# In-place recurrence operands, and a last layer without the meta tokens' own rows, in a two-layer hybrid encoder on Trainium2

## The chip, the cores and the metric

The program runs on one core of one Trainium2 chip. The metric is the device time in microseconds (us); lower is better. Engines: PE is TensorE (matmuls; PEld its weight loads), DVE VectorE, ACT ScalarE, POOL GpSimd, SP SyncE, which here issues every DMA.

## The reference

512 tokens of width 1024, with 16 learned meta tokens in front (T = 528), pass through two layers. The meta rows of the last layer's output are dropped.

```python
h = jnp.concatenate([meta, x], axis=1)                  # 528 rows
for l in range(DEPTH):                                   # 2 layers
    u = rmsnorm(h, norm_g[l])
    p = u @ w_in[l]                                      # 1024 -> 9216
    hq, hf_f, hf_b, hi, hgt, aq, ak, av, agt = jnp.split(p, split_idx, axis=-1)
    o_h = hgrn2_mixer(hq, hf_f, hf_b, hi, hgt, lbs[l], hg_norm_g[l])
    o_a = diff_attention_mixer(aq, ak, av, agt, diff_lambda[l], diff_subln_g[l], l, cos, sin)
    h = h + jnp.concatenate([o_h, o_a], axis=-1) @ w_out[l]
out = rmsnorm(h, final_norm_g)[:, N_META:]
```

`hgrn2_mixer` is a gated linear recurrence, S_t = diag(f_t) S_{t-1} + k_t v_t^T, o_t = S_t^T q_t, run forwards and backwards over the 528 rows with 8 heads of 128x128 state, k = (1-lb) sigmoid(-z) and f = lb + (1-lb) sigmoid(z). `diff_attention_mixer` is dense attention with 8 heads, each the difference of two softmaxes (components of 64), with rotary positions. Both outputs are normalised and gated.

## The kernel before

Activations stand transposed: features on the 128 partitions, the 528 tokens along the free axis. The work of a layer is cut into **units**, output tiles of 128 features (`layer_units`, L69): per recurrent head zf, zb, q, v, g, per attention head aq, ak, av, ag, and then the output projection in outA, outB and outC. A unit is 8 **pieces** (one per 128 input features); a piece (L1130) is six matmuls in fp32r, for three products of high and low parts of weight and activation (`w_hi*u_hi`, `w_hi*u_lo`, `w_lo*u_hi`), each in two halves of 264 tokens. ACT rounds a weight tile to its high part (L507), POOL takes the rest (L437).

The 16 heads of a layer run one after another, 13 steps each (0 to 12). All five engines have a program of their own written out step by step, and semaphores between them. At each step PE does the head's own matmuls and is then **fed** a set number of pieces of the next head's units (`feed`, L1170; `HG_FEED`, L103, and `AT_FEED`, L104). ACT evacuates a finished unit (`evacuate`, L550) and then rounds the weights of a later one; DVE follows it up (`follow`, L851: for zf and zb L885 and L887 form the gate f; for aq and ak L897 to L905 apply the rotation).

A **recurrent head** has no chunks of 16. Its 528 rows are scored in 8 levels: level 0 is the diagonal, and level lv >= 1 is, within blocks of 2m rows, m = 2^(lv-1), the scores between the two halves of a block. At PE step s, `level` (L1200) does level s-1: four pairs of 128x128 fp32 matmuls (L1210, each two instructions) on keys and queries from `qk_dec`, and for levels 0 to 4 a small 16x16 one for the meta rows (L1207). DVE prepares each level in `level_products` (L938). `decay` holds four rows of running products of gates, two for queries and two for keys:

```python
step(dve.tensor_tensor(block_half(dst, m, 1), block_half(qkk_c[:, 0:3:2, :], m, 1), block_half(decay[:, 0:2, :], m, 1), ALU.mult))
dve.tensor_tensor(block_half(dst, m, 0), block_half(qkk_c[:, 0:2, :], m, 0), block_half(decay[:, 2:4, :], m, 0), ALU.mult)
totals = step(dve.tensor_tensor(totals[...], block_totals(slice(0, 3), m, 0), block_totals(slice(0, 3), m, 1), ALU.mult))
second = step(dve.tensor_tensor(second, second, spread(slice(0, 2), 0), ALU.mult))
firsts = step(dve.tensor_tensor(firsts, firsts, spread(slice(1, 3), 1), ALU.mult))
```

So per level there are two products (L950, L954), the next totals of the gates (L963) and two spreads that widen `decay` (L972, L974); `copy_level` (L916, L922) puts the level's scores under a mask into `score`. The last products are 1056 wide (L1045, L1050). The starting values of `decay` come from ACT (`set_decay`, L541 and L542) and POOL (L447, L448). Level lv's products wait for level lv-2's matmuls, since `qk_dec` has two buffers. Steps 9 to 12 turn the keys, form and chain the states (L976, L987) and compute the outputs (L1274 to L1282); step 12 waits for `mixed` of the head before, which `gate_meta` (L1023) releases.

An **attention head** goes through five chunks of queries, four of 128 rows and one of the 16 meta rows, two components each. At steps 0 to 9 PE forms the scores (L1300, L1302), DVE the maximum (L1064), ACT the exponential (L660), and the next scores wait for it. DVE then combines the two components (`p`, L1092), PE transposes (L1329, L1330) and multiplies by the values (L1315, L1317), ACT reads out and squares. `scale_output` (L1002) multiplies the rows of the head before by the inverse root from POOL (L1006, and L1009 for the meta rows), PE turns them back (L1218, L1222), and `gate_main` and `gate_meta` gate them.

Of the kernel before, what the change touches and what calls it, by code (L numbers as in the profile page):

```python
# [31 lines left out]
P = 128  # L32
DEPTH = 2
# [19 lines left out]
AT_TILES = ("aq", "ak", "av", "ag")  # L53
STAGE_USE = {"zf": 0, "zb": 1, "g": 2, "aq": 0, "ak": 1, "ag": 2}
# [44 lines left out]
HG_STEPS = LEVELS + 5  # L99
AT_STEPS = 2 * 6 + 1  # L100
DECAY_STEP = TURN_KEYS + 1
# [58 lines left out]
def unit_of(tile):  # L160

    return next(i for i, u in enumerate(UNITS) if u[0] == "outB" and u[2] == tile)

# [33 lines left out]
def encoder_trunk(nc, x_t, w_units, norm_g, lb_logits, hg_gain, lambdas, at_gain, final_g,  # L197
# [12 lines left out]
    with ctx:  # L210
# [30 lines left out]
        totals = sb("totals", [P, 3, TOTALS])  # L241
        decay = sb("decay", [P, 4, T])
        qkk = sb("qkk", [P, 2, 3, T])
        qk_dec = sb("qk_dec", [P, 2, 2, T])

# [47 lines left out]
        decay_set = sem("decay_set")  # L293
        qk_ready = sem("qk_ready")
        level_done = sem("level_done")
# [81 lines left out]

        def u_out(k):

            if k < 4:  # L380
                return decay[:, k, N_META:T]
            return qkk[:, (k - 4) // 2, (k - 4) % 2, N_META:T]
# [41 lines left out]
        def _(pool):  # L424
# [16 lines left out]
            def set_decay(l, c):  # L441
                g = l * HG_HEADS + c
                if g > 0:
                    pool.wait_ge(qk_ready, 10 * g)
                if c == 0:
                    pool.wait_ge(h_sq_summed, l + 1)
                pool.memset(decay[:, 1, :], 1.0).then_inc(decay_set, 1)  # L447
                pool.memset(decay[:, 3, :], 1.0).then_inc(decay_set, 1)  # L448

# [11 lines left out]
            def cut_mixed(n):  # L461
                pool.wait_ge(mix_hi_ready, n + 1)
                pool.tensor_tensor(mix_lo[:, n % 8, :], mixed_t[:, :],  # L463
                                   mix_hi[:, n % 8, :].bitcast(f32), ALU.subtract)\
                    .then_inc(mix_lo_ready, 1)
# [3 lines left out]
            for l in range(DEPTH):  # L469
# [7 lines left out]
                set_decay(l, 0)  # L477
                follow(range(len(HG_TILES)))
                for c in range(HEADS):
                    n = l * HEADS + c  # L480
                    for s in range(steps_of(c)):
                        if s == mix_step(c) and c > 0:
                            cut_mixed(n - 1)
                        if s == DECAY_STEP and c + 1 < HG_HEADS:
                            set_decay(l, c + 1)
                        follow(units_after(c, s))
# [7 lines left out]
        def _(act):  # L494
# [15 lines left out]
            def square_h(n, k):  # L510
# [13 lines left out]
                act.activation(decay[:, k % 4, :], h[:, tile, :], ACT.Square).then_inc(h_sq, 1)  # L524

            def root(n):

                act.wait_ge(h_sq_summed, n + 1)
                act.activation(two(sq[:, :]), pair[:, :, both], ACT.Sqrt, bias=eps_count[:, :])\
                    .then_inc(root_ready, 1)  # L530
# [4 lines left out]

            def set_decay(l, c):
                g = l * HG_HEADS + c
                act.wait_ge(stage_read, 3 * (l * HEADS + c) + 2)
                if g > 0:
                    act.wait_ge(qk_ready, 10 * g)  # L540
                act.activation(decay[:, 0:4:2, :], gate_f[:, 0:2, :], ACT.Copy).then_inc(decay_set, 1)  # L541
                act.activation(gate_f[:, 2, :], gate_f[:, 0, :], ACT.Copy).then_inc(decay_set, 1)  # L542
# [7 lines left out]
            def evacuate(l, i):  # L550
# [3 lines left out]
                src = proj[t % 2][:, :, both]  # L554
                act.wait_ge(unit_done, t + 1)
                if what not in ("outA", "outB", "outC"):
# [5 lines left out]
                    a, b = two(stage[:, use % 2, 0, :]), two(stage[:, use % 2, 1, :])  # L562
                    done = evacuated[t % 2]
                    if what in ("zf", "zb"):
# [8 lines left out]
                        act.activation(qkk[:, c % 2, 1 + d, :], stage[:, use % 2, 1, :], ACT.Copy,  # L573
                                       scale=one_minus_lb[:, l, row:row + 1]).then_inc(k_scaled, 1)
                    elif what == "q":
                        act.activation(two(qkk[:, c % 2, 0, :]), src, ACT.Copy).then_inc(done, 1)
# [21 lines left out]
            def scale_output(n):  # L598

                act.wait_ge(o_inv_ready, n + 1)  # L600
                for j in range(N_CHUNKS + 1):
# [3 lines left out]
                    if j < N_CHUNKS:  # L605
# [9 lines left out]

            def hgrn(l, c, s):
# [16 lines left out]
                if s == HG_STEPS - 1:  # L633
                    if n > 0:
                        act.wait_ge(o_turned, 2 * n)
                    act.wait_ge(o_done, g + 1)
                    step(act.activation(o_rows[:, 0:N_CHUNKS, :],
                                        main[:, :].rearrange("p (c n) -> p c n", c=4), ACT.Copy))
                    act.activation(o_rows[0:N_META, N_CHUNKS, :], meta[0:N_META, 0:P], ACT.Copy)\
                        .then_inc(o_taken, 1)  # L640
                    act.wait_ge(o_taken, n + 1)
                    for j in range(N_CHUNKS + 1):
# [4 lines left out]
                        if j < N_CHUNKS:  # L647
# [4 lines left out]
            def attend(l, c, s):  # L652
                n, a = l * HEADS + c, l * AT_HEADS + c - HG_HEADS
                i, comp = s // 2, s % 2
                if i < 5:
                    rows = P if i < 4 else N_META
                    if comp == 0 and i >= 2:
                        act.wait_ge(p_ready, a * 5 + i - 1)
                    act.wait_ge(max_ready, a * 10 + 2 * i + comp + 1)
# [5 lines left out]
                if comp == 0 and 2 <= i < 7:  # L665
                    j = i - 2
                    rows = P if j < 4 else N_META
                    if j == 0:
                        act.wait_ge(o_turned, 2 * n)
                        act.wait_ge(mix_lo_ready, n)  # L670
                    act.wait_ge(pv_done, a * 5 + j + 1)
                    inv = row_inv[0:rows, j % 2, 0:1]
                    act.activation(o_rows[0:rows, j, :], meta[0:rows, 0:P], ACT.Copy, scale=inv)\
                        .then_inc(pv_read if j < 4 else o_taken, 1)
                    if j < 4:
                        act.wait_ge(pv_read, a * 4 + j + 1)
                    else:
# [3 lines left out]
                                   accum_out=o_sums[0:rows, j:j + 1]).then_inc(act_step if j < 4 else sq_ready, 1)  # L681
                    if j < 4:
# [3 lines left out]
                if comp == 1 and 1 <= i < 6:  # L686
                    j = i - 1
                    rows = P if j < 4 else N_META
                    act.wait_ge(p_turned, a * 5 + j + 1)
# [15 lines left out]
            def round_mixed(l, c):  # L705
# [5 lines left out]
                act.activation(mix_hi[:, c % 8, :], mixed_t[:, :], ACT.Copy).then_inc(mix_hi_ready, 1)  # L711
# [10 lines left out]
            for l in range(DEPTH):  # L722
# [6 lines left out]
                for i in range(len(HG_TILES)):  # L729
                    evacuate(l, i)  # L730
                    if i == 2:
                        set_decay(l, 0)
                for c in range(HEADS):
                    for s in range(steps_of(c)):
# [5 lines left out]
                        if s == DECAY_STEP and c + 1 < HG_HEADS:  # L740
                            set_decay(l, c + 1)
# [21 lines left out]
        def _(dve):  # L763
# [53 lines left out]
            def add_squares(n, k):  # L817
# [4 lines left out]
                dve.tensor_tensor(sq[:, :], decay[:, 0, :] if k == 1 else sq[:, :], decay[:, k % 4, :],  # L822
                                  ALU.add).then_inc(h_sq_added, 1)

            def invert_roots(n):
                dve.wait_ge(root_ready, n + 1)
                after(step(dve.reciprocal(sq[:, :], sq[:, :])))
# [23 lines left out]
            def follow(l, i):  # L851
# [4 lines left out]
                if what in ("outA", "outB"):  # L856
                    dve.wait_ge(unit_done, t + 1)
                    dve.tensor_tensor(two(h[:, j, :]), two(h[:, j, :]), proj[t % 2][:, :, both], ALU.add)\
# [4 lines left out]
                if what == "outC":  # L863
                    for tile in range(EARLY_TILES):
# [4 lines left out]
                        else:  # L869
                            dve.wait_ge(unit_done, t + 1)  # L870
                        dve.tensor_tensor(two(h[:, tile, :]), two(h[:, tile, :]),
                                          last_out(l, tile)[:, :, both], ALU.add)\
# [7 lines left out]
                a, b = stage[:, use % 2, 0, :], stage[:, use % 2, 1, :]  # L880
# [8 lines left out]
                elif what == "g":  # L889
                    dve.tensor_tensor(gates[:, c % 2, :], a, b, ALU.mult).then_inc(stage_read, 1)  # L890
                elif what == "ag":
                    dve.scalar_tensor_tensor(gates[:, c % 2, :], a, 1.0, b, ALU.add, ALU.mult)\
                        .then_inc(stage_read, 1)
                else:
# [4 lines left out]
                    step(dve.tensor_tensor(a, a, cos_sin[:, 0, :], ALU.mult))  # L899
                    w = step(dve.tensor_tensor(b, b, cos_sin[:, 1, :], ALU.mult))  # L900
# [4 lines left out]
                    dve.tensor_tensor(gate_f[:, d, :], a, b, ALU.add).then_inc(stage_read, 1)  # L905
# [30 lines left out]
            last_decay = {}  # L936
# [505 lines left out]
```

## Time and profile before

| | |
|---|---|
| median of 3 runs | 1691.0 us (1689.66 to 1691.99) |
| the profiled execution | 1691.08 us, of which 1689.3 us are the span of the trace |
| mean granted PE clock | 0.981 |
| busy: PE, PEld, DVE, ACT, POOL | 1554.6, 1514.3, 1188.7, 754.1, 567.1 us |

The span runs from the first to the last instruction in the trace. Matmuls are pipelined, so the distance between starts tells what one costs and not the length of a row. Line numbers with an L are those of the kernel before.

### The profile page before, as it was taken

What the parts mean: (1) busy time and instruction counts of PE and PEld (TensorE: products, weight loads), DVE (VectorE), ACT (ScalarE), POOL (GpSimd) and SP (SyncE); (2) the same over time, 40 slices, a digit from 0 to 9 for tenths busy, and PEclk for the clock granted to TensorE, in tenths of its full rate; (3) what the DMA queues carried; (4) which work ended last, traced back from release to release, by engine and by line L of the source; (5) the groups of instructions that cost most, each with busy time, mean ns of one, the idle gap of its engine ahead of it and who ended that gap; (6) DMA issues with size and microseconds to landing.
All of it is one profiled execution on the core that took longest, in us unless ns stands there. A gap on an engine that the chain in (4) does not pass through costs nothing.

```text
span 1689.3 us, 30863 instructions
## 1 busy us (share of the span) xinstructions
PE 1554.6 (92%) x12616; PEld 1514.3 (90%) x12616; DVE 1188.7 (70%) x1871; ACT 754.1 (45%) x1712; POOL 567.1 (34%) x319
## 2 busy tenths in 40 slices
PE   5999999999999999999989999999999999999996
PEld 5999998999999999998888899899889999999985
DVE  6888888888734666665468888888895356666655
ACT  5343433333434556655343344343335346665542
POOL 3334332334234333332433333333233233333331
PEclk8999999999999999999999999999999999999998
DMA  4211111111212222222221111111112122222211
GB/s 148 86 51 63 51 51 51 63 51 51 64 63 89 64 74 65 64 64 64 75 76 52 62 51 51 63 51 50 51 51 76 62 90 64 63 72 68 72 56 62
DMA packets 34492, 109.57 MB, mean 65 GB/s; under 512 B 4912, under 2 KB 5040, under 8 KB 34352
## 3 DMA queue, kind: packets, MB, share of 16 engines
q1 hardware_dynamic: 34352, 107.61, 19.9%
q8 instruction: 100, 1.64, 0.4%
q14 instruction: 40, 0.33, 0.1%
HBM read 96.84 MB, written 2.10 MB: 59 GB/s over the span
## 4 chain that ended last, share of the span: by engine, by line
PE 62%; DVE 27%; issue 9%; ACT 1%; POOL 1%; DMA 0%; DVEq 0%; SPq 0%; ACTq 0%
PE proj L1149 41%; DVE qk_dec L954 5%; PE meta L1315 3%; DVE decay L972 3%; PE pair L1210 3%; DVE score L922 3%; DVE stage L885 2%; PE pair L1300 2%; DVE qk_dec L950 2%; PE pair L1302 2%; PE main L1329 2%; DVE o_rows L1009 2%; DVE decay L974 2%; DVE totals L963 2%; PE main L1274 1%
## 5 line engine op out<-in xcount | busy, mean ns | idle before, releaser
L437 POOL TENSOR_TENSOR w_lo<-w_raw,w_hi 128x1024 fp32r<-128x1024 f32 x178 | 453.4, 2548 | 804.1 <-ACT w_hi L507 800.9
L1149 PE MATMUL proj<-u_hi,w_hi 128*128 128x264 f32 x2304 | 503.7, 300 | 15.2 <-DVE u_lo L841 15.2
L1149 PE MATMUL proj<-u_lo,w_hi 128*128 128x264 f32 x2304 | 471.5, 286 | 0.0
L1149 PE MATMUL proj<-u_hi,w_lo 128*128 128x264 f32 x2304 | 471.2, 286 | 0.0
L1149 PEld LDWEIGHTS proj<-u_hi,w_hi 128*128 128x128 f32 x2304 | 360.8, 192 | 18.5 <-issue 16.3
L1149 PEld LDWEIGHTS proj<-u_lo,w_hi 128*128 128x128 f32 x2304 | 361.5, 191 | 0.0
L1149 PEld LDWEIGHTS proj<-u_hi,w_lo 128*128 128x128 f32 x2304 | 360.2, 190 | 0.0
L1064 DVE TENSOR_REDUCE neg_max<-pair 128x1 f32<-128x528 f32 (+1 forms) x160 | 112.3, 702 | 248.6 <-PE pair L1302 248.6
L660 ACT ACTIVATE decay<-pair,neg_max 128x528 f32<-128x528 f32 (+1 forms) x160 | 111.9, 699 | 289.7 <-DVE neg_max L1064 289.7
L507 ACT ACTIVATE w_hi<-w_raw 128x1024 fp32r<-128x1024 f32 x178 | 186.4, 1048 | 13.3 <-PE proj L1149 8.8
L1210 PE MATMUL pair<-qk_dec 128*128 128x128 f32 x896 | 131.8, 292 | 4.2 <-DVE score L922 4.2
L950 DVE TENSOR_TENSOR qk_dec<-qkk,decay 128x528 f32<-128x528 f32 (+1 forms) x112 | 89.4, 799 | 58.0 <-PE meta L1282 51.2
L1210 PEld LDWEIGHTS pair<-qk_dec 128*128 128x128 f32 x896 | 114.3, 199 | 7.8 <-DVE qk_dec L954 4.6
L1149 PE MATMUL proj<-mix_hi,w_hi 128*128 128x264 f32 x496 | 105.3, 293 | 9.4 <-issue 4.7
L463 POOL TENSOR_TENSOR mix_lo<-mixed_t,mix_hi 128x528 fp32r<-128x528 f32 x32 | 42.2, 1319 | 203.9 <-ACT mix_hi L711 203.9
L954 DVE TENSOR_TENSOR qk_dec<-qkk,decay 128x528 f32<-128x528 f32 (+1 forms) x112 | 108.1, 965 | 0.0
L569 ACT ACTIVATE stage<-proj 128x528 f32<-128x528 f32 x32 | 19.6, 611 | 197.6 <-PE proj L1149 197.6
L1149 PE MATMUL proj<-mix_hi,w_lo 128*128 128x264 f32 x496 | 100.8, 285 | 0.0
L1149 PE MATMUL proj<-mix_lo,w_hi 128*128 128x264 f32 x496 | 100.7, 284 | 0.0
L1300 PE MATMUL pair<-k_stack,q_stack 128*128 128x264 f32 (+1 forms) x320 | 86.4, 290 | 13.5 <-ACT decay L660 13.5
L1149 PEld LDWEIGHTS proj<-mix_hi,w_hi 128*128 128x128 f32 x496 | 76.6, 189 | 12.1 <-issue 6.7
L1315 PE MATMUL meta<-v_main,cols 128*128 128x128 f32 x640 | 85.9, 277 | 0.0
(186 smaller groups left out, 2615.2 us busy)
## 6 DMA issues: line engine op xcount, KB each, us to landing
w_raw<-w_units SPq DMA_DIRECT2D x178, 512.0 KB, 3.4
k_stack<-k_stack SPq DMA_DIRECT2D x32, 132.0 KB, 2.3
q_stack<-gate_f SPq DMA_DIRECT2D x32, 132.0 KB, 2.4
h<-x_t SPq DMA_DIRECT2D x8, 264.0 KB, 4.3
out_t<-decay SPq DMA_DIRECT2D x4, 256.0 KB, 2.1
out_t<-qkk SPq DMA_DIRECT2D x4, 256.0 KB, 2.1
cos_sin<-rope SPq DMA_DIRECT2D x1, 528.0 KB, 5.4
masks<-level_masks SPq DMA_DIRECT2D x1, 448.0 KB, 4.6
```

Of the source, the lines that this page charges most:

```text
L437: pool.tensor_tensor(w_lo[:, u % N_CUT, :, :], w_raw[:, u % N_RAW, :, :], w_hi[:, u % N_CUT, :, :].bitcast(f32), ALU.subtract)\
L507: act.activation(w_hi[:, u % N_CUT, :, :], w_raw[:, u % N_RAW, :, :], ACT.Copy)\
L660: act.activation(two(decay[0:rows, 2 * (i % 2) + comp, :]), pair[0:rows, :, both], ACT.Exp, bias=neg_max[0:rows, i % 2, comp:comp + 1], ac ...
L922: dve.copy_predicated(score[:, :, :], mask, src).then_inc(level_read, 1)
L950: step(dve.tensor_tensor(block_half(dst, m, 1), block_half(qkk_c[:, 0:3:2, :], m, 1), block_half(decay[:, 0:2, :], m, 1), ALU.mult))
L954: dve.tensor_tensor(block_half(dst, m, 0), block_half(qkk_c[:, 0:2, :], m, 0), block_half(decay[:, 2:4, :], m, 0), ALU.mult).then_inc(qk_r ...
L972: last_decay["second"] = step(dve.tensor_tensor(second, second, spread(slice(0, 2), 0), ALU.mult))
L1064: dve.tensor_reduce(neg_max[0:rows, i % 2, comp:comp + 1], pair[0:rows, :, both], axis=mybir.AxisListType.XY, op=ALU.max, negate=True)\
L1149: ins = pe.matmul(proj[t % 2][:, n, both], w, x[:, k, cols_n], start=(k == 0 and p == 0), stop=(k == last_k and p == 2))
L1210: ins = pe.matmul(pair[:, lv % 2, j * P:(j + 1) * P], k[:, chunk(j)], q[:, chunk(j)], start=True, stop=True)
L1300: pe.matmul(pair[0:rows, b, both], q_stack[:, comp, cs], k_stack[:, comp, keys], start=True, stop=False)
L1315: pe.matmul(meta[:, 0:P], cols[:, kk, :], v_main[:, kk, :], start=(kk == 0), stop=False)
```

## The change

Three things. **(1)** The four rows of `decay` and `set_decay` go. The operands of a head stand in `ops` (forward keys KF, backward keys KB, and two rows of queries, QB and QF, both already multiplied by their own gates) and are widened in place: per level DVE does one multiply on the keys and one on the queries, each with a total spread over the half that needs it. Because the keys are widened ahead of the level, ACT first copies that level's keys out (`copy_keys`, into `k_level`), while the queries are read by the level's matmuls straight from `ops`, with a stride pattern that takes alternately m columns of QB and m of QF (`halves_of`). Totals have two rows, not three. **(2)** In the last layer, units whose result is needed for real tokens only (`REAL_ONLY`: q, g, aq, ag and the output projection) are computed for 512 columns, in one matmul of 512 in place of two of 264; keys, values and gates of recurrence stay at 528. **(3)** In the last layer the meta rows' own queries go: the 16x16 level matmuls and their copies, their outputs, the fifth chunk of attention, and their gating.

The diff, cut to its core:

```diff
+REAL_ONLY = ("q", "g", "aq", "ag", "outA", "outB", "outC")
+KF, KB, QB, QF = range(4)
+TURNS = LEVELS - 1
+def short(l, what):
+    return l == LAST and what in REAL_ONLY
+def query_chunks(l):
+    return N_CHUNKS + (l < LAST)
...
-        qkk = sb("qkk", [P, 2, 3, T])
+        ops = sb("ops", [P, 2, 4, T])
+        q_raw = qk_dec[:, 1, 0, :]
+        k_sum = qk_dec[:, 1, 1, :]
+        k_level = qk_dec[:, 0, :, :]
...
+        def halves_of(c, first, m, cols_at, n):
+            at = ops[:, c % 2, first, cols_at:cols_at + n]
+            return bass.AP(tensor=at.tensor, offset=at.offset,
+                           ap=[[8 * T, P], [2 * m, n // (2 * m)], [T + m, 2], [1, m]])
...
-            def set_decay(l, c):
...
+            def copy_keys(g, c, lv):
+                if lv > 1:
+                    act.wait_ge(k_widened, g * TURNS + lv - 1)
+                else:
+                    act.wait_ge(k_scaled, 2 * (g + 1))
+                if lv > 2:
+                    act.wait_ge(level_done, g * LEVELS + lv - 1)
...
+                act.activation(dst, halves_of(c, KF, m, first, T - first), ACT.Copy).then_inc(k_copied, 1)
...
             def hgrn(l, c, s):
+                if s == 0:
+                    copy_keys(g, c, 1)
                 if s == 1:
                     copy_diagonal(g)
+                if 2 <= s <= TURNS:
+                    copy_keys(g, c, s)
...
-            def level_products(g, c, lv, copied=None):
...
+            def start_operands(l, c):
+                dve.tensor_tensor(k_sum, ops[:, c % 2, KF, :], ops[:, c % 2, KB, :], ALU.add)
...
+                step(dve.tensor_tensor(ops[:, c % 2, QB, :], q_raw, gate_f[:, 1, :], ALU.mult))
+                dve.tensor_tensor(ops[:, c % 2, QF, :], q_raw, gate_f[:, 0, :], ALU.mult)
+            def widen_keys(g, c, lv):
+                dve.wait_ge(k_copied, g * TURNS + lv)
...
+                keys = moved_halves(c, KF, m)
+                dve.tensor_tensor(keys, keys, facing_totals(m, KF), ALU.mult).then_inc(k_widened, 1)
+            def widen_queries(g, c, lv):
+                dve.wait_ge(level_done, g * LEVELS + lv + 1)
+                queries = moved_halves(c, QB, m)
+                dve.tensor_tensor(queries, queries, facing_totals(m, QB), ALU.mult).then_inc(qk_ready, 1)
...
+                elif s == 1:
+                    widen_keys(g, c, 1)
+                    total_pairs(1)
+                elif s <= LEVELS:
+                    lv = s - 1
+                    widen_queries(g, c, lv)
+                    if lv < TURNS:
+                        widen_keys(g, c, lv + 1)
+                    copy_level(g, lv)
+                    if lv < TURNS:
+                        total_pairs(lv + 1)
+                    if lv == META_LEVELS - 1 and l < LAST:
                         copy_meta_levels(g)
-                elif s == LEVELS:
...
                 for w, x, p in ((wh, hi, 0), (wh, lo, 1), (wl, hi, 2)):
-                    for n, cols_n in enumerate(halves):
-                        ins = pe.matmul(proj[t % 2][:, n, both], w, x[:, k, cols_n],
+                    for n, cols_n in enumerate((slice(N_META, T),) if short(l, what) else halves):
+                        out = proj[t % 2][:, n, 0:SEQ if short(l, what) else HALF]
+                        ins = pe.matmul(out, w, x[:, k, cols_n],
...
+                    return k_level[:, lv % 2, at:at + n], halves_of(c, QB, 2 ** (lv - 1), at, n)
+                if lv < META_LEVELS and l < LAST:
+                    k, q = operands(0, N_META)
+                    pe.matmul(meta[0:N_META, lv * N_META:(lv + 1) * N_META], k, q, start=True, stop=True)
...
+                if n // HEADS < LAST:
+                    step(ins)
+                    rows = o_rows[0:N_META, N_CHUNKS, :]
+                    ins = dve.tensor_scalar(rows, rows, o_inv[0:N_META, N_CHUNKS:N_CHUNKS + 1], None, ALU.mult)
...
-                if i < 5:
+                if i < chunks:
                     row_max(a, i, comp)
```

## Rows read from the trace of the kernel before

**Rows 1.** The page, busy time: us (share of the span), x instructions.

```profile
PE 1554.6 (92%) x12616; PEld 1514.3 (90%) x12616; DVE 1188.7 (70%) x1871; ACT 754.1 (45%) x1712; POOL 567.1 (34%) x319
PE 62%; DVE 27%; issue 9%; ACT 1%; POOL 1%; DMA 0%; DVEq 0%; SPq 0%; ACTq 0%
```

**Rows 2.** Who waited for whom: us in total, times, longest us.

```profile
PE meta L1207 <- DVE score L922: 39.6, 18, 2.6
...
PE pair L1240 <- DVE score L922: 8.3, 6, 1.4
...
PE pair L1210 <- DVE score L922: 4.2, 2, 2.1
```

**Rows 3.** Windows after stalls: length, busy of five engines, then granted clock.

```profile
72.00:77.00 5.00, 5.00 (x30) 4.98 (x29) 5.00 (x11) 0.74 (x2) 0.00 (x0) 0.66 0.00 0
...
1147.00:1152.00 5.00, 4.35 (x26) 4.34 (x27) 5.00 (x10) 0.21 (x1) 0.00 (x0) 0.66 0.00 0
...
187.00:188.00 1.00, 1.00 (x11) 1.00 (x10) 0.98 (x2) 0.00 (x0) 0.62 (x2) 1.00 0.00 0
```

**Rows 4.** Groups by line on DVE: busy us, mean ns, then idle before.

```profile
L950 DVE TENSOR_TENSOR qk_dec<-qkk,decay 128x528 f32<-128x528 f32 (+1 forms) x112 | 89.4, 799 | 58.0 <-PE meta L1282 51.2 <-ACT gate_f L542 5.0 <-PE pair L1210 1.7
L922 DVE COPY_PREDICATED score<-masks,pair 128x512 f32<-128x512 int32 x112 | 81.7, 729 | 1.6
L972 DVE TENSOR_TENSOR decay<-decay,totals 128x528 f32<-128x528 f32 (+1 forms) x96 | 66.2, 689 | 0.0
...
L963 DVE TENSOR_TENSOR totals<-totals 128x396 f32<-128x396 f32 (+2 forms) x96 | 26.9, 281 | 0.0
```

**Rows 5.** Timeline of a recurrent head around the stall: start us, us, engine, what.

```profile
211.85 2.37 POOL L437 TENSOR_TENSOR w_lo<-w_raw,w_hi 128x1024 fp32r<-128x1024 f32 x1 [5.58 <-ACT w_hi L507]
...
211.86 2.65 DVE L885 TENSOR_SCALAR stage<-stage,one_minus_lb,lb 128x528 f32<-128x528 f32 x1
...
218.41 0.20 PE L1207 MATMUL meta<-qk_dec 128*16 128x16 f32 x2 [2.65 <-DVE score L922]
...
239.82 0.62 ACT L542 ACTIVATE gate_f<-gate_f 128x528 f32<-128x528 f32 x1
```

**Rows 6.** Timeline of PE in that head: a level with L1207, then one without.

```profile
205.06 0.40 PE L1149 MATMUL proj<-u_hi,w_lo 128*128 128x264 f32 x2
...
206.45 0.49 PE L1149 MATMUL proj<-u_hi,w_hi 128*128 128x264 f32 x2
...
226.87 0.41 PE L1149 MATMUL proj<-u_hi,w_lo 128*128 128x264 f32 x2
...
227.93 0.49 PE L1149 MATMUL proj<-u_hi,w_hi 128*128 128x264 f32 x2
```

**Rows 7.** Chain in order of time, one attention head: start us, us, what.

```profile
1443.41 2.20 PE proj L1149 x18
...
1447.57 2.34 DVE o_rows L1009
...
1475.63 0.89 PE meta L1315 x8
1476.53 0.22 PE meta L1317 x2
...
1478.21 0.35 PE main L1329 x4
```

**Rows 8.** Timeline of that head: PE's waits and DVE ahead of the transposes.

```profile
1450.04 0.63 PE L1218 MATMUL main<-ident,o_rows 128*128 128x128 f32 x4 [0.71 <-DVE o_rows L1009]
...
1472.23 0.30 PE L1300 MATMUL pair<-k_stack,q_stack 128*16 128x264 f32 x1 [1.02 <-ACT decay L660]
1472.73 0.60 PE L1329 MATMUL main<-ident,qk_dec 128*128 128x128 f32 x4
...
1469.98 0.71 DVE L905 TENSOR_TENSOR gate_f<-stage 128x528 f32<-128x528 f32 x1
...
1471.73 0.77 DVE L1092 SCALAR_TENSOR_TENSOR qk_dec<-decay,row_inv 128x528 f32<-128x528 f32 x1
```

More of the change, by code:

```diff
@@ L162, in unit_of, with before, turned @@
     return next(i for i, u in enumerate(UNITS) if u[0] == "outB" and u[2] == tile)
+def short(l, what):
+    return l == LAST and what in REAL_ONLY
+def query_chunks(l):
+    return N_CHUNKS + (l < LAST)
+def before(a, full, per):
+    return full * min(a, LAST * per) + (full - 1) * max(a - LAST * per, 0)
+def turned(n):
+    return before(n, 2, HEADS)
 def units_left(c):
@@ L376, in block_totals, with grown, rows_of, tokens @@
             return src.rearrange("p a (b h) -> p a b h", h=2)[:, :, :, half]
+        def grown(l, what, bank):
+            return bank[:, 0, 0:SEQ] if short(l, what) else bank[:, :, both]
+        def rows_of(l, what, x):
+            return x[:, N_META:T] if short(l, what) else two(x)
+        def tokens(l, what):
+            return slice(N_META if short(l, what) else 0, T)
+        def normed(n):
+            return slice(N_META if n == DEPTH else 0, T)
+        def normed_halves(n):
+            return ((0, slice(0, SEQ), normed(n)),) if n == DEPTH else \
+                tuple((b, both, keys) for b, keys in enumerate(halves))
         def u_out(k):
@@ L553, in evacuate @@
                 t = l * LAYER_UNITS + i
-                src = proj[t % 2][:, :, both]
+                src = grown(l, what, proj[t % 2])
                 act.wait_ge(unit_done, t + 1)
@@ L561, in evacuate @@
                         act.wait_ge(stage_read, use - 1)
-                    a, b = two(stage[:, use % 2, 0, :]), two(stage[:, use % 2, 1, :])
+                    a, b = (rows_of(l, what, stage[:, use % 2, x, :]) for x in range(2))
                     done = evacuated[t % 2]
@@ L600, in scale_output @@
                 act.wait_ge(o_inv_ready, n + 1)
-                for j in range(N_CHUNKS + 1):
+                chunks = query_chunks(n // HEADS)
+                for j in range(chunks):
                     rows = P if j < N_CHUNKS else N_META
@@ L826, in invert_roots @@
                 dve.wait_ge(root_ready, n + 1)
-                after(step(dve.reciprocal(sq[:, :], sq[:, :])))
+                after(step(dve.reciprocal(sq[:, normed(n)], sq[:, normed(n)])))
             def norm_u(l):
@@ L857, in follow @@
                     dve.wait_ge(unit_done, t + 1)
-                    dve.tensor_tensor(two(h[:, j, :]), two(h[:, j, :]), proj[t % 2][:, :, both], ALU.add)\
+                    sums = rows_of(l, what, h[:, j, :])
+                    dve.tensor_tensor(sums, sums, grown(l, what, proj[t % 2]), ALU.add)\
                         .then_inc(evacuated[t % 2], 1)
@@ L1164, in last_piece @@
                 for w, x, p in ((wh, mix_hi, 0), (wh, mix_lo, 1), (wl, mix_hi, 2)):
-                    for n, cols_n in enumerate(halves):
-                        ins = pe.matmul(last_out(l, tile)[:, n, both], w, x[:, EARLY_K, cols_n],
+                    for n, cols_n in enumerate((slice(N_META, T),) if l == LAST else halves):
+                        out = last_out(l, tile)[:, n, 0:SEQ if l == LAST else HALF]
+                        ins = pe.matmul(out, w, x[:, EARLY_K, cols_n],
                                         start=(p == 0), stop=(p == 2))
```

315 lines of the change are left out of this document (161 added, 154 removed).

## The prediction

> **What bounds the kernel now.** First the busy times and the shares of the chain that ended last [rows 1]: PE is busy for 1554.6 of 1689.3 us, and 62% of the chain is PE's, but 27% is DVE's. So almost any matmul taken away shortens the run, and there are places where DVE holds PE up. The waits name them [rows 2]: PE waits for the score copy L922 at a level (L1207 39.6 us, L1210 4.2) and ahead of the key transposes (L1240, 8.3), 52.1 us together. Next the timeline [rows 5]: in a recurrent head PE stands 2.65 us before level 4. A step of PE there takes 3.4 us. DVE's step before the change has two products, two spreads, a copy and a total: 4 x 0.69 + 0.73 + 0.28 = 3.8 us, the products priced like the spreads, without the waits for POOL that raise their mean [rows 4], so DVE falls behind at every level, and then zf's follow-up waits behind POOL's cut (L885 took 2.65 us beside a POOL instruction of 2.37 us that began at the same time, [rows 5]). That is the stall. A stall costs twice: in windows of 5 us behind eleven of PE's stalls the granted clock is 0.66, which is 2.4 GHz for a third of the window and 1.2 GHz for the rest; nine of them follow a wait for L922 [rows 3] (the first and the last of the nine stand there).
>
> **Part 1, operands in place.** Per level DVE loses two of its four 528-wide multiplies (0.69 each, [rows 4]), and the 1056-wide ones at the end. Its step becomes 2 x 0.69 + 0.73 + 0.2 = 2.3 us against PE's 3.4, or 3.1 in the last layer where L1207 goes. The path of a level is now: level done, queries widened (0.7), next level. PE's fed pieces in between last 2.2 us, 18 matmuls [rows 7], which covers it. The keys run a level ahead: widened, copied by ACT (0.62 by the 528-wide copy, [rows 5]), read two PE steps later; about 1.5 us of work inside 6. ACT gains 7 x 0.62 a head and loses `set_decay`; at 754.1 us busy [rows 1] it has room, and the copies stand ahead of that step's evacuations in its order. POOL loses two memsets. No DMA is added.
>
> So the 52.1 us go, except where POOL's cut still falls into DVE's path. I place it for zf. POOL holds DVE until 214.22 [rows 5]. Then come a total (0.2), zf's two instructions (1.0) and the queries (0.7): 216.2, while level 4 is due at 215.76 (218.41 less 2.65). That leaves 0.4 us a head. In the last layer levels come due 4 x 0.34 = 1.4 sooner and the cut, two levels in, 0.7 sooner, so about 1.0. Head 7 of each layer has fewer pieces to cover with; I put 2 us there. Residue: 7 x 0.4 + 7 x 1.0 + 2 x 2 = 14. Bounds: nothing, or a whole POOL instruction of 2.4 in all 16 heads, 38. **Gain 52 - 14 = 38 us.** Shorter stalls did not lower the clock: the waits at L1240 are up to 1.4 us [rows 2], and the window behind one of them has 1.00 [rows 3]. So the nine slow windows go as well: 9 x 5 x 0.34 = **15 us**; none of it if the stalls stay above 2 us. Head 7's wait for `mixed` ahead of its outputs stays: the follow-up of ak and the state chain end last there, and neither changes.
>
> A new cost has no row: the moving operand of levels 1 to 7 is read with a stride. The nearest rows read contiguously: 8 instructions in 0.89, 0.111 each [rows 7]. I take no extra, since 0.111 is already twice the time of 128 columns at 2.4 GHz (0.053), and keep as bounds zero and a doubling of level 1, whose columns alternate one by one: 8 x 0.111 x 16 = 14 us. The Trainium skill ("SBUF — State Buffer", "Door 1: The DMA port swizzle") says that SBUF has 16-byte lines and that an access pattern wants two hits on a line before it moves on; by that level 1 alone would pay, and no run here shows it yet.
>
> **Part 2, 512 columns at once.** In the last layer q, g, aq, ag (32 units), outA (8) and the rest of the output projection have 384 pieces, so 1152 pairs of 264 become single matmuls of 512. A pair costs 2 x 0.122 = 0.244 (2.20 for 18, [rows 7]); 264 columns at 2.4 GHz are 0.110, so 0.012 lies on top of each matmul. If that is per matmul, 512 columns take 0.225 and a pair saves 0.019; if it grows with the columns, 0.237 and 0.007; if it vanishes, 0.213 and 0.031. I take the first, because the fp32 rows with another column count lie 0.004 above twice their column time and not the same 11% [rows 7], which doesn't look like a rate: **22 us**, ends 8 and 36. The Trainium skill ("TensorE: Matmul & The Clock Gate", "Back-to-back issue gap") has columns over 2.4 GHz plus 2.5 ns; the pitch of 0.122 is already above that (0.1125), and by the page's rule this term would be 1152 x 0.009 = 11 us.
>
> **Part 3, no meta queries in the last layer.** In 8 recurrent heads: five L1207 each. From the last weight product before a level to the first after it are 1.39 us with L1207 and 1.06 without [rows 6]: 40 x 0.33 = 13. L1281 and L1282, 4 instructions of 0.111, 8 x 0.44 = 3.5. The turn L1222 goes in 16 heads: 1.8. Sum **18 us**. In 8 attention heads: the value product of chunk 4, ten instructions (0.89 + 0.22, [rows 7]), 1.1; its transposes, 0.35 [rows 7]; the wait of 0.71 for L1009, which a POOL instruction stretches to 2.34 and which goes altogether [rows 7, 8]. The scores of chunk 4 and the wait of 1.02 before them [rows 8] do **not** go in full: the transposes then wait for `p` of chunk 3, and L1092 stands behind the rotation of ak, whose L905 ends at 1470.6. Without the maximum between them L1092 ends 0.6 to 0.8 sooner, so 0.75 of the step is gained. Sum 2.9 a head, **23 us**. The stacked operands of the next head are next in line; nine pieces and a value product, 7.7 us [rows 7], still cover their rounding and their DMAs. I take nothing for it, and 1 us a head as the bound.
>
> **Sum.** 38 + 15 + 22 + 18 + 23 = 116 us off 1691.1, the profiled execution, which agrees with the median of 1691.0: 1575 us.
>
> **Rivals.** (A) The DVE stall stays under another name: POOL's cut blocks the queries at most heads, each level waits, and the clock keeps falling. For it: both new multiplies read two tensors of SBUF, the kind that waited for POOL. Against it: 1.1 us of slack per step where there was none. Part 1 then brings some 10 us of its 53: 1618. (B) PE takes the strided queries slowly at level 1 only: 1589. (C) Slower than before: the strided operand slows all seven levels. These are the 896 instructions L1210, 0.111 each; the gain of 116 us is eaten from 0.129 on top of each, 2.2 times its price, and at three times it the run takes 1575 + 199 = 1774. For it: no moving operand before is strided. Against it: an instruction has 0.111 for 128 columns; from m = 4 on the runs are four elements and more. (D) The change isn't what it says: the long matmuls gain nothing (the clock or the pitch of 512 is worse), while the rest holds: 1597.
>
> **How the numbers follow.** The forecast 0.62, A 0.18, B 0.06, D 0.08, C 0.04, and 0.02 for no change by some loop of waits over the ACT copies. Best end: no residue (-14) and 0.213 a matmul (-14), 1547. Far end: A with the pitch at its bad end, 1632; leaving the last of A out, the range is 1545 to 1625. About 0.2% (3 us) is what a measurement of this kernel can tell from no change: faster 0.94, within 0.02, slower 0.04.
>
> **What would show it.** Right: PE instructions fall to about 11,150 (1152 pairs merged, some 310 meta matmuls gone); DVE busy to about 920; no wait of PE for `score` above 1.5 us, and the clock near 0.99; last-layer attention heads 3.8 us closer together (2.9 and 48 pairs of 0.019). A 512-wide matmul starts 0.225 after the one before. Wrong: rows of PE waiting for `ops` or `k_level` at each level (A); level 1 longer than levels 2 to 7 (B); all levels longer than 1.06 between pieces (C).

## The result, and the profile after

The changed kernel takes **1587.16 us** (median of 4 runs, 1586.62 to 1587.52), the kernel before on the same chip 1690.33 (1689.16 to 1691.99): a ratio of 0.9389, 95% interval 0.9372 to 0.9405. That is 103 us less, where 116 were forecast. The span of the profiled execution is 1585.3 us, the mean granted clock 0.988. Line numbers below are those of the kernel whose profile is shown.

The page of the changed kernel, busy times and then the chain that ended last, against [rows 1]:

```profile
PE 1496.3 (94%) x11148; PEld 1412.5 (89%) x11148; DVE 986.5 (62%) x1542; ACT 772.8 (49%) x1689; POOL 533.2 (34%) x287
...
PE 76%; DVE 13%; issue 6%; ACT 2%; DMA 1%; POOL 1%; SPq 1%; DVEq 0%; ACTq 0%; POOLq 0%
```

DVE's share of the chain fell from 27% to 13%: the end now hangs on PE more than before. Its waits (us in total, times, longest), against [rows 2]:

```profile
PE main L1440 <- DVE qk_dec L1189: 10.0, 14, 1.2
PE pair L1411 <- ACT decay L743: 9.0, 10, 2.0
...
PE pair L1316 <- DVE ops L1065: 4.9, 8, 0.7
...
PE main L1381 <- DVE state_f L1087: 2.6, 1, 2.6
PE main L1381 <- DVE mixed_t L1127: 2.6, 1, 2.6
...
PE meta L1313 <- DVE ops L1065: 1.3, 7, 0.2
```

The 52.1 us for the score copy are gone. In their place stand 6.2 us for the widened queries (L1065), in fifteen waits of at most 0.7, and 10.0 us in which the transposes wait for `p` (L1189); before, that wait (L1329 for L1092) came to 1.6.

The timeline of the changed kernel, three stretches of it (start us, us, engine, what, and in brackets the wait before): a recurrent head of layer 0, one of the last layer, and an attention head of the last layer.

```profile
56.73 1.16 PE L1316 MATMUL pair<-qk_dec 128*128 128x128 f32 x8
57.64 0.49 PE L1247 MATMUL proj<-u_hi,w_hi 128*128 128x264 f32 x2
...
60.16 1.57 PE L1316 MATMUL pair<-ops,qk_dec 128*128 128x128 f32 x8
61.43 0.55 PE L1247 MATMUL proj<-u_hi,w_hi 128*128 128x264 f32 x2
...
64.03 1.23 PE L1316 MATMUL pair<-ops,qk_dec 128*128 128x128 f32 x8
65.00 0.49 PE L1247 MATMUL proj<-u_hi,w_hi 128*128 128x264 f32 x2
...
66.91 2.37 POOL L509 TENSOR_TENSOR w_lo<-w_raw,w_hi 128x1024 fp32r<-128x1024 f32 x1 [7.15 <-ACT w_hi L568]
...
67.24 2.19 DVE L1030 TENSOR_TENSOR totals<-totals 128x132 f32<-128x132 f32 x1
...
67.51 1.16 PE L1316 MATMUL pair<-ops,qk_dec 128*128 128x128 f32 x8
...
68.43 0.49 PE L1247 MATMUL proj<-u_hi,w_hi 128*128 128x264 f32 x2
...
71.04 0.21 PE L1313 MATMUL meta<-ops,qk_dec 128*16 128x16 f32 x2 [0.19 <-DVE ops L1065]
...
867.28 2.49 POOL L509 TENSOR_TENSOR w_lo<-w_raw,w_hi 128x1024 fp32r<-128x1024 f32 x1 [6.50 <-ACT w_hi L568]
...
867.44 2.62 DVE L969 TENSOR_SCALAR stage<-stage,one_minus_lb,lb 128x528 f32<-128x528 f32 x1
870.10 0.43 DVE L971 TENSOR_SCALAR gate_f<-stage 128x528 f32<-128x528 f32 x1
870.45 0.70 DVE L1065 TENSOR_TENSOR ops<-ops,totals 128x528 f32<-128x528 f32 x1
...
871.21 1.16 PE L1316 MATMUL pair<-ops,qk_dec 128*128 128x128 f32 x8 [0.68 <-DVE ops L1065]
...
879.16 0.39 PE L1247 MATMUL proj<-u_lo,w_hi 128*128 128x512 f32 x1
...
880.79 0.39 PE L1247 MATMUL proj<-u_hi,w_lo 128*128 128x512 f32 x1
...
1341.88 2.37 DVE L983 TENSOR_TENSOR stage<-stage,cos_sin 128x528 f32<-128x528 f32 x1
...
1346.05 0.77 DVE L1189 SCALAR_TENSOR_TENSOR qk_dec<-decay,row_inv 128x528 f32<-128x528 f32 x1
...
1346.96 0.63 PE L1440 MATMUL main<-ident,qk_dec 128*128 128x128 f32 x4 [1.22 <-DVE qk_dec L1189]
```

Four things are to be read here. **Levels:** from a level's start to the next piece are 0.91 us at level 0 (56.73 to 57.64), 1.27 at level 1, 0.97 at level 2 and 0.92 at level 3. From the start of level 1 to that of level 2 are 3.87 (60.16 to 64.03). **The collision:** POOL's cut still falls on DVE in both layers, on the totals in layer 0 (2.19 for an operation of 0.3) and on zf's follow-up in the last layer (2.62, as L885 in [rows 5]); the queries follow (L1065), and PE waits 0.19 and 0.68 where it had waited 2.65. **The long matmul:** from 879.16 to 880.79 are seven steps from one matmul of 512 columns to the next, 0.233 us each. **Attention:** the rotation of ak stands ahead of `p` on DVE, drawn out to 2.37 by POOL, and the transposes wait 1.22.

The windows with a low granted clock, beside [rows 3] (length, busy of PE, PEld, DVE, ACT, POOL, then clock, DMA share, GB/s):

```profile
410.00:415.00 5.00, 4.01 (x22) 4.04 (x23) 4.52 (x7) 2.60 (x5) 1.32 (x1) 0.66 0.33 74
820.00:831.00 11.00, 6.35 (x30) 6.38 (x31) 10.93 (x15) 4.45 (x7) 0.00 (x0) 0.53 0.14 48
1195.00:1200.00 5.00, 4.97 (x26) 4.83 (x27) 3.77 (x4) 2.42 (x4) 1.27 (x1) 0.66 0.48 107
1513.00:1518.00 5.00, 4.70 (x26) 4.15 (x25) 2.02 (x5) 2.32 (x6) 1.27 (x1) 0.66 0.03 11
```

Besides the first microseconds and the end, these are all. Adding up one minus the clock over windows of 1 us, again without start and end, gives 22.2 us before and 10.25 after, 12 us less. (What a slow window costs depends on where it falls, see e4.)

DVE's groups by line (busy us, mean ns, idle before), against [rows 4]:

```profile
L1065 DVE TENSOR_TENSOR ops<-ops,totals 128x528 f32<-128x528 f32 (+1 forms) x96 | 97.6, 1017 | 34.8 <-PE pair L1316 34.2
...
L1057 DVE TENSOR_TENSOR ops<-ops,totals 128x528 f32<-128x528 f32 (+1 forms) x96 | 70.9, 739 | 0.0
L1030 DVE TENSOR_TENSOR totals<-totals 128x264 f32<-128x264 f32 (+2 forms) x96 | 68.7, 716 | 0.0
```

An undisturbed L1065 takes 0.70 (the row at 870.45), as 82 of these 96 do within 0.02; the other 14 take 2.87, each beside a cut of POOL. L1030 would have a mean of 0.23 undisturbed. So 96 x 0.32 + 96 x 0.48 = 77 us of these two lines are time in which DVE stood behind POOL, somewhat more than the 66 by which DVE's 986.5 us exceed the 920 forecast. What that forecast counted of such waits was not written down. POOL's cuts held DVE up before the change too, on other lines (L885 and L954 were 39 and 31 us over their undisturbed time). PE pays for almost none of it.

### The profile page after: what moved, and what is told of

Read it like the earlier page. It is cut to its first block, busy times and chain, and to the rows that moved or that the text cites. A ratio compares the mean times of both kernels' runs of the same rounds, so it can differ in the third digit from the quotient of the medians.

```text
span 1585.3 us, 27727 instructions
## 1 busy us (share of the span) xinstructions
PE 1496.3 (94%) x11148; PEld 1412.5 (89%) x11148; DVE 986.5 (62%) x1542; ACT 772.8 (49%) x1689; POOL 533.2 (34%) x287
## 3 DMA queue, kind: packets, MB, share of 16 engines
q1 hardware_dynamic: 34352, 107.61, 21.9%
## 4 chain that ended last, share of the span: by engine, by line
PE 76%; DVE 13%; issue 6%; ACT 2%; DMA 1%; POOL 1%; SPq 1%; DVEq 0%; ACTq 0%; POOLq 0%
PE proj L1247 51%; PE pair L1316 7%; PE meta L1426 3%; PE pair L1411 2%; PE pair L1413 2%; PE main L1440 2%; DVE stage L969 1%; PE main L1381 1%; DVE totals L1030 1%; PE main L1382 1%; DMA q_stack<-gate_f 1%; PE pair L1362 1%; DVE neg_max L1160 1%; DVE o_rows L1104 1%; PE main L1323 1%
## 5 line engine op out<-in xcount | busy, mean ns | idle before, releaser
L1247 PE MATMUL proj<-u_hi,w_hi 128*128 128x264 f32 (+1 forms) x2048 | 497.0, 314 | 15.2 <-DVE u_lo L923 15.2
L1247 PE MATMUL proj<-u_hi,w_lo 128*128 128x264 f32 (+1 forms) x2048 | 466.8, 300 | 0.0
L1247 PE MATMUL proj<-u_lo,w_hi 128*128 128x264 f32 (+1 forms) x2048 | 466.8, 299 | 0.0
L568 ACT ACTIVATE w_hi<-w_raw 128x1024 fp32r<-128x1024 f32 x178 | 186.6, 1049 | 22.2 <-DMA w_raw<-w_units 11.9
L689 ACT ACTIVATE qk_dec<-ops 128x528 f32<-128x528 f32 (+1 forms) x112 | 75.8, 677 | 126.1 <-DVE ops L1057 126.1
L1316 PE MATMUL pair<-ops,qk_dec 128*128 128x128 f32 x896 | 130.2, 289 | 4.9 <-DVE ops L1065 4.9
L1316 PEld LDWEIGHTS pair<-ops,qk_dec 128*128 128x128 f32 x896 | 116.1, 191 | 9.5 <-DVE ops L1065 7.0
L1065 DVE TENSOR_TENSOR ops<-ops,totals 128x528 f32<-128x528 f32 (+1 forms) x96 | 97.6, 1017 | 34.8 <-PE pair L1316 34.2
L1247 PE MATMUL proj<-mix_hi,w_hi 128*128 128x264 f32 (+1 forms) x372 | 103.6, 333 | 8.3 <-issue 3.9
L1247 PE MATMUL proj<-mix_lo,w_hi 128*128 128x264 f32 (+1 forms) x372 | 99.7, 322 | 0.0
L1247 PE MATMUL proj<-mix_hi,w_lo 128*128 128x264 f32 (+1 forms) x372 | 99.6, 322 | 0.0
L1411 PE MATMUL pair<-k_stack,q_stack 128*128 128x264 f32 x288 | 78.8, 294 | 10.2 <-ACT decay L743 9.0
L1006 DVE COPY_PREDICATED score<-masks,pair 128x512 f32<-128x512 int32 x112 | 82.7, 738 | 0.0
```

What stands on the lines that cost most here:

```text
L568: act.activation(w_hi[:, u % N_CUT, :, :], w_raw[:, u % N_RAW, :, :], ACT.Copy)\
L689: act.activation(dst, halves_of(c, KF, m, first, T - first), ACT.Copy).then_inc(k_copied, 1)
L1006: dve.copy_predicated(score[:, :, :], mask, src).then_inc(level_read, 1)
L1065: dve.tensor_tensor(queries, queries, facing_totals(m, QB), ALU.mult).then_inc(qk_ready, 1)
L1247: ins = pe.matmul(out, w, x[:, k, cols_n], start=(k == 0 and p == 0), stop=(k == last_k and p == 2))
L1316: ins = pe.matmul(pair[:, lv % 2, j * P:(j + 1) * P], k, q, start=True, stop=True)
```

## The experiments

Each ratio is to the kernel before, run beside it on the same chip (medians 1690.3 to 1692.1). The 1587.16 us of the changed kernel come from runs apart from these, so a difference from them in us is good to about 2. The runs e1 to e4 share a chip, and so do e5 to e7, and e8 and e9.

### e1: operands in place alone

```diff
-LAST = DEPTH - 1
+LAST = DEPTH
```

> The in-place operands alone: both layers keep the meta rows' queries and the halves of 264. Theory (what layer 0 of the changed kernel shows holds in both layers): its recurrent heads end 29.5 us sooner, twice that is 59, so about 1631 us. The prediction's own terms for this part, 38 + 15 = 53, give 1637. Rival (the gain came mainly from the shorter last layer): above 1655.

Measured: **1633.0 us** (1632.23 to 1633.96), ratio 0.9653 [0.9639, 0.9668]: 58.6 us less than before. Its waits for the queries:

```profile
PE meta L1313 <- DVE ops L1065: 2.7, 14, 0.3
...
PE pair L1316 <- DVE ops L1065: 0.3, 2, 0.2
```

The stalls of 52.1 us shrank to 3.0, and the low windows between start and end from 22.2 us to 5.1: 49 + 17 us, of which 7 go back to the stride (e3). That makes 59.

### e2: all units at 528 columns

```diff
 def short(l, what):
-    return l == LAST and what in REAL_ONLY
+    return False
```

The last pieces of four output tiles keep their 512 columns (12 of the 1152 matmuls), while the sums of all tiles are read in halves of 264, so the values of those four tiles change; the amount of work does not.

> The changed kernel with the matmuls of 512 columns undone (two of 264 over all 528 tokens in the last layer again; everything else as changed). Theory (512 columns start 0.233 us apart, a pair of 264 takes 0.244): 1152 x 0.011 = 13 us slower than the changed kernel, 1600. The prediction's term, 22 us: 1609. If the long matmuls gain nothing: 1587.

Measured: **1598.34 us** (1597.83 to 1601.48), ratio 0.9454 [0.9439, 0.947]. Against the changed kernel the 512 columns bring 11.2 us, half of the 22 forecast; by the pitch in the timeline, 1152 x (0.244 - 0.233) = 13. Not all of that reaches the end: by the starts of their transposes the attention heads of the last layer are 37.26 us apart here and 37.09 in the changed kernel, so 48 pairs bring 0.17 us where the pitch gives 0.53. Against e1 the meta tokens' own rows bring 34.7 us.

### e3: queries without the stride

```diff
-                    return k_level[:, lv % 2, at:at + n], halves_of(c, QB, 2 ** (lv - 1), at, n)
+                    return k_level[:, lv % 2, at:at + n], ops[:, c % 2, QB, at:at + n]
```

> The changed kernel, but the levels' matmuls read the backward queries in one contiguous row in place of alternating pieces of two rows; this leaves half of each level's decay out of the scores. Theory (the stride costs 0.36 us at level 1, 0.06 at level 2, nothing above, 16 heads): 6.7 us faster than the changed kernel, 1580. The prediction's value (no cost): 1587. If a strided operand costs something at every level that hides in the pitch: below 1575.

Measured: **1579.91 us** (1579.12 to 1580.33), ratio 0.9339 [0.9325, 0.9353]: the stride costs 7.3 us. Its timeline at levels 1 and 2:

```profile
59.33 1.16 PE L1316 MATMUL pair<-ops,qk_dec 128*128 128x128 f32 x8
60.24 0.49 PE L1247 MATMUL proj<-u_hi,w_hi 128*128 128x264 f32 x2
...
62.76 1.16 PE L1316 MATMUL pair<-ops,qk_dec 128*128 128x128 f32 x8
63.67 0.49 PE L1247 MATMUL proj<-u_hi,w_hi 128*128 128x264 f32 x2
```

Both levels take 0.91 us again. So single columns in turn cost 0.36 us a level up to the next piece, pairs 0.06; level 3, in runs of four, had 0.92 already with the stride. That would be 16 x 0.42 = 6.7. The pieces behind level 1 were slower as well: from the start of level 1 to that of level 2 are 3.43 us here (59.33 to 62.76) and 3.87 with the stride. That is 0.44 (0.42 in the last layer, and nothing in its head 7), and with level 2 the 16 heads come to 7.4 us, the measured 7.3.

### e4: the kernel before, with the follow-ups one step later

Here, in the kernel before, the follow-ups of the recurrent heads 0 to 6, those of zf and zb among them, come one step later, which was to take zf's away from POOL's cut.

```diff
+    elif c < HG_HEADS:
+        units = [*units_after(c, s - 1)]
     elif not HG_HEADS < c < HEADS - 1:
```

> The kernel before with one thing moved: the follow-up of zf and zb on DVE comes one step later. Theory (DVE's work per step, 3.8 us, is more than PE's 3.4, so the backlog comes back a level later): the waits of PE for the score copy stay above 35 of 52 us in total and the time above 1675. Rival (only the collision with POOL's cut makes the stall): the waits go, and with the clock they cost 67 us: about 1625.

Measured: **1703.41 us** (1701.75 to 1703.97), ratio 1.0068 [1.0053, 1.0083]: 12 us slower. Its waits:

```profile
PE pair L1242 <- DVE score L924: 32.3, 14, 2.3
PE pair L1212 <- DVE score L924: 21.0, 28, 2.1
...
PE meta L1209 <- DVE score L924: 3.5, 4, 1.3
```

They come to 56.8 us, no less than the 52.1. The timeline of a head shows what happens (layer 0):

```profile
207.10 2.90 DVE L956 TENSOR_TENSOR qk_dec<-qkk,decay 128x528 f32<-128x528 f32 x1
...
215.01 4.97 POOL L439 TENSOR_TENSOR w_lo<-w_raw,w_hi 128x1024 fp32r<-128x1024 f32 x1 [5.58 <-ACT w_hi L509]
...
218.29 1.98 DVE L887 TENSOR_SCALAR stage<-stage,one_minus_lb,lb 128x528 f32<-128x528 f32 x1
...
222.73 1.13 PE L1212 MATMUL pair<-qk_dec 128*128 128x128 f32 x8 [0.38 <-DVE score L924]
...
237.63 0.63 PE L1242 MATMUL pair<-ident,qk_dec 128*128 128x128 f32 x4 [2.31 <-DVE score L924]
```

The same product in the same head of the kernel before:

```profile
203.94 2.90 DVE L954 TENSOR_TENSOR qk_dec<-qkk,decay 128x528 f32<-128x528 f32 x1
```

The move did not free DVE of POOL. The product was held for 2.90 before as well, and zf's follow-up, now behind the start of the cut at 215.01, still takes 1.98 where it takes 0.55 undisturbed. PE meets the debt later, the largest part (2.31) ahead of the key transposes. So the stall is not tied to zf's place. How long it would be with the backlog and no collision no run shows; that collisions alone don't make it, the changed kernel shows, where operations of DVE are held just so (2.19 and 2.87 above) and PE waits 0.2 to 0.7.

The longer waits account for 4.7 of the 12 us at most. Where the 12 lie is seen in the distances between the key transposes of two heads. In the kernel before they are 48.8 to 49.2 us (the first and the last head of a layer aside), whether a window of low clock falls between them or not: a head with one had no wait at L1240, and a head without one waited 1.4 there for a DVE that was still behind. In e4 the windows come behind the key transposes (here one of them):

```profile
238.00:243.00 5.00, 5.00 (x32) 4.98 (x31) 2.12 (x3) 0.68 (x2) 1.02 (x2) 0.66 0.00 0
```

There they add to the time: heads with one are 50.4 to 50.8 us apart and heads without one 48.9 to 49.0. The eight heads with such a window that are longer than the same heads before (by 1.2 to 1.8 each) make up 11.5 of the 12 us.

### e5: the same move in the changed kernel

```diff
+    elif c < HG_HEADS:
+        units = [*units_after(c, s - 1)]
     elif not HG_HEADS < c < HEADS - 1:
```

> The changed kernel with the same move as in the run before: zf and zb followed up one step later. Theory (DVE now has slack, 2.3 us of work in a step of 3.1 to 3.4, so what is left of the stall is only the collision with POOL's cut): the 7 waits of 0.19 and the 7 of 0.67 for the queries go, 6 us, to about 1581. Rival (no slack, as before the change): the same or slower, 1587 to 1600.

Measured: **1579.8 us** (1578.58 to 1580.64), ratio 0.9336 [0.9322, 0.935]: 7.4 us less than the change. PE's waits for the widened queries fell from 6.2 us to one of 0.2, and the profile lost 3.4 us less to low clock. POOL still holds DVE up (the totals of 128x132 take 2.20 in layer 0, as before the move). The same edit costs 12 us where DVE is behind and gains 7 where it has slack, so the stall needs the backlog.

### e6: ak's rotation moved too

On top of e5, ak's follow-up moves from step 7 to step 8 in the attention heads, behind `p`.

```diff
-    elif s % 2 == 1:
+    elif s == 8:
+        units = [*units_after(c, 5), *units_after(c, 6)]
+    elif s % 2 == 1 and s != 7:
```

> As the run before it, and in attention heads the follow-up of ak comes after the combination of the two components of step 8 in place of before it. Theory (PE's waits of 1.02 in the first layer and 1.22 in the last are for DVE work that stands behind the rotation): 6 x 1.0 and 6 x 1.2 go as well, 13 us, to about 1568. Rival (the stacked operands of the next head come later by what is gained): 1578 to 1590.

Measured: **1577.8 us** (1575.31 to 1579.37), ratio 0.9321 [0.9305, 0.9337]: 2 us less than e5, with ranges that overlap, where 13 were expected. By the starts of the transposes the last layer's heads are 36.1 us apart instead of 37.1, but those of layer 0 are 40.35 instead of 40.0. In layer 0 the meta tokens' fifth chunk is still there, and the timeline shows it wait:

```profile
569.72 0.75 DVE L985 STREAM_SHUFFLE stage<-stage 128x528 f32<-128x528 f32 x1
...
572.50 0.69 DVE L1164 TENSOR_REDUCE neg_max<-pair 16x1 f32<-16x528 f32 x1
573.22 0.69 ACT L747 ACTIVATE decay<-pair,neg_max 16x528 f32<-16x528 f32 x1 [3.06 <-DVE neg_max L1164]
...
574.69 1.16 PE L1430 MATMUL meta<-v_main,cols 128*128 128x128 f32 x8 [1.03 <-ACT cols L781]
```

The rotation now stands ahead of the fifth chunk's maximum (L1164). ACT waits 3.06 us for that maximum, and only behind its exponential (L747) does it copy the turned `p` of the chunk before (L781), which PE's value product needs. Beside that, this profile lost 3.4 us more to low clock than e5's (21.2 against 17.8): 7 x 1.0 - 6 x 0.35 - 3.4 = 1.5.

### e7: level 1 from a dense copy

On top of e6, DVE writes level 1's queries side by side into a buffer of their own.

```diff
+        q_first = sb("q_first", [P, T])
...
+                dve.tensor_copy(q_first[:, :].rearrange("p (b h m) -> p b h m", h=2, m=1), halves_of(c, QB, 1, 0, T))
...
+                    if lv == 1:
+                        return k_level[:, 1, at:at + n], q_first[:, at:at + n]
```

> As the run before it, and the queries of level 1 are copied into one contiguous row by DVE while it idles at the start of a head, so that PE reads level 1 without a stride. Theory (0.36 us in 16 heads are the stride's cost and the copy lies in idle time): 5.8 us less than the run before it. Rival (the copy delays the first level by about 0.7 in each head, 11 us): 5 us more than the run before it.

Measured: **1568.25 us** (1567.38 to 1569.16), ratio 0.9268 [0.9254, 0.9282]: 9.6 us less than e6. Level 1 in its timeline:

```profile
59.74 1.16 PE L1325 MATMUL pair<-q_first,qk_dec 128*128 128x128 f32 x8
60.65 0.49 PE L1254 MATMUL proj<-u_hi,w_hi 128*128 128x264 f32 x2
```

0.91 us: the 0.36 are gone, 16 x 0.36 = 5.8 us. By the starts of levels 1 and 2, which are 3.43 us apart again, it is 6.4. No cost of the copy on DVE shows, though eight of the 16 copies last 2.57 us in place of 0.51. The rest is mostly clock in the two profiles: two slow windows in a row at 1188 to 1196 us in e6's, 3.4 us, have no counterpart here. Executions whose mean clock was the same (0.993) differ by 7 to 9 us.

### e8 and e9: the later rotation in the last layer alone

```diff
-    elif s == 8:
+    elif l == LAST and s == 8:
         units = [*units_after(c, 5), *units_after(c, 6)]
-    elif s % 2 == 1 and s != 7:
+    elif s % 2 == 1 and (l < LAST or s != 7):
```

> The kernel of e7 with the later follow-up of ak in the last layer alone; layer 0's attention heads follow up at step 7 again, as the change has them. Theory: in e6 the move paid in the last layer (a head about 1 us shorter, where the transposes waited for p) and cost 0.33 us a head in layer 0, where PE then waited for ACT's copies of the meta rows; so layer 0's heads come back to 40.0 us, 6 x 0.33 = 2 us less than e7, about 1566. Rival: layer 0's lengthening in e6 was not the move's but the clock's (it lost 3.4 us more than e5 in its profile), and then this kernel takes e7's time within 1 us, 1568.

e9 is e7 once more, beside it:

> The kernel of e7 once more, on the same chip as e8, for the comparison: 1568 by both theories.

Measured: e8 **1566.42 us** (1566.09 to 1567.59), ratio 0.9259 [0.9246, 0.9271]; e9 1568.48 (1567.87 to 1569.15), ratio 0.9272 [0.9259, 0.9284]. The 2.1 us are the 2 that six heads of layer 0 were to give back, and their starts are 40.03 us apart again. So the move itself lengthened layer 0, not the clock: behind the first 28 us both profiles lost the same to it (12.2 us each). e8 is the fastest version here, 20.7 us under the change, and leaves nothing out.

## Why the prediction was right, and where its sizes were off

The mechanism and the sign held; the sum was 13 us too large. It came that near with some luck, since 8 us more from the stalls cover a third of what the other terms were too large by. The terms, with what was measured:

| term | forecast | measured |
|---|---|---|
| stalls | 38 | 45.9 (52.1 - 6.2) |
| clock | 15 | 12 |
| 512 columns | 22 | 11.2 (e2) |
| meta rows, recurrent | 18 | 16.4 |
| meta rows, attention | 23 | 21.9 |
| stride | 0 | -7.3 (e3) |

Attention: heads of the last layer are 40.0 us apart in e1 and 37.26 in e2, which differ in the meta rows alone; 2.74 times 8. Recurrent: e1 and e2 differ by 34.7, less 21.9, plus the 3.6 us by which e2's waits for the queries (6.6) are longer than e1's (3.0), since such waits stand in the first row. The sum is 100.1 of 103; the last 3 us are not assigned.

- **Stalls.** Right in kind and place: POOL's cut ahead of zf's follow-up is still there, and the queries stand behind it. The residue was put at 0.4, 1.0 and 2 (head 7) and is 0.19, 0.68 and at most 0.16. In layer 0 the cut falls on the totals instead of zf, and zf then takes 0.55; the 2 us for head 7 had no row. Its long wait ahead of the outputs (2.65, L1381) stayed, as said.
- **Clock.** No slow window stands behind a level any more. One new one is behind PE's wait of 2.0 us for the exponential (L1411), in the last head, and the layer boundary has one window more than before. "A stall costs twice" was not right as a mechanism, though: within a head of the kernel before, a slow window cost next to nothing beside the stall (e4, 48.8 to 49.2 us with and without one). The 38 and the 15 are one sum, what PE lost to a DVE that was behind, and only their sum can be checked: 53 forecast, 58 measured. Nor does each such wait bring a slow window: before, nine of the 16 waits for L922 of more than 2 us have one behind them.
- **The step that failed: 512 columns.** "I take the first, because the fp32 rows with another column count lie 0.004 above twice their column time and not the same 11%": fp32 rows of 128 columns were the wrong neighbour for a long fp32r matmul. The pitch is 0.233, 0.020 above the 0.213 of 512 columns at 2.4 GHz, while 264 columns lie 0.012 above theirs, so most of the excess grows with the columns, and a pair saves 0.011, not 0.019. The near end of the bounds (8) was closer than the value taken. The Trainium skill ("TensorE: Matmul & The Clock Gate", "Back-to-back issue gap") has the columns' time plus 2.5 ns, for a matmul by itself, 0.216 for 512: both pitches here lie above it. That the 11 us by that rule are what e2 measured is luck, because it is off by 0.017 for the long one and by 2 x 0.0095 for the pair, and the two errors cancel.
- **Stride.** "I take no extra, since 0.111 is already twice the time of 128 columns": wrong at level 1 and, by little, at level 2, right from level 3 on. Rival B had the place, and half of its price (7 of 14 us). The Trainium skill ("SBUF — State Buffer", "Door 1: The DMA port swizzle") wants two hits on a 16-byte line before the pattern moves on; the 0.36 with one column at a time agree with it, and the 0.06 with two are more than the nothing that it would have there.
- **Attention.** The wait for `p` behind the rotation was named, and it came: 1.22 and 0.30 in each head. POOL's cut draws L983 out to 2.37 just ahead of it, and 2.74 a head were gained, not 2.9. e6 and e8 moved the rotation and got 1.0 a head back.
- **Signs.** 11148 PE instructions against about 11,150; a clock of 0.988 against 0.99; no wait above 0.7 for the levels. Heads 2.96 closer, not 3.8, and DVE at 986.5, not 920: its busy time holds its waits for POOL. Rivals A (1618) and C (1774) are refuted by these rows, D by the pitch and e2.

## What to carry to other kernels

An engine that needs more time per step than the engine it feeds accumulates debt, and moving one piece of its work away from a collision then only moves the stall (e4, +12 us); first cut its work per step, and after that the same move pays (e5, -7). Waits and low clock can stand for the same lost time: compare the distances of heads with and without a slow window before you count both. When a chunk of work is taken out of a loop, look at the order behind it: the follow-up that suited five chunks cost 1 us a head with four, and the better order for four cost 0.35 a head with five. Price a new shape by the nearest row of the same type and length, and a strided operand of PE by the length of its runs.

## What the runs showed of the hardware that was not expected

- Eight 128-column fp32 instructions take 0.36 us longer when the moving operand alternates between two rows after each column (0.44 by the start of the next level), 0.06 when after two, and 0.01 or nothing from four on. ACT's copies of the keys read two rows in the same way: 0.86 to 0.88 us at level 1, 0.68 to 0.75 at level 2, 0.63 to 0.65 at levels 3 and 4 (L689, 528 columns). DVE shows no such cost: e7's copy of level 1's queries, the same pattern as PE's, takes 0.51 us undisturbed, and the multiplies L1065, which read one row in runs of two, four or eight with gaps between them and then the other, take 0.70 like the spreads of [rows 4] (0.69).
- The excess of an fp32r matmul over its columns at 2.4 GHz is 0.012 us for 264 columns and 0.020 for 512.
- PE's wait of 2.0 us for the exponential was followed by a window at 0.66; behind the one of at most 1.4 in [rows 3] the clock had stayed at 1.00. It is not so each time: the profile of e2 has two waits of 2.5 and 2.6 us (L1381) with no slow window behind them.
